# Retention, one core: the last head's totals and the first two tiles of the output projection in another order on TensorE

## The reference

```
def _mixer_retention(h, cos, sin, w_in, w_out):
    q, k, v, g = jnp.split(h @ w_in, SPLIT_RET, axis=-1)
    ...
    o = (scores of q and k, weighted by a decay) @ v, for 4 heads of 512 values
    ...
    o = _rms_noaffine(o).reshape(B, T, 2 * D_MODEL).astype(h.dtype)
    return (jax.nn.silu(g) * o) @ w_out
```

## Time and profile before

| what | us |
|---|---|
| three timed runs, median (lowest, highest) | 3081.69 (3080.63, 3082.3) |
| the profiled execution, its own time | 3077.38 |
| its span in the profile | 3075.6 |
| TensorE's matrix products, busy | 2896.1 (94%) |
| VectorE, ScalarE busy | 1446.9, 1105.1 |
| mean granted clock of TensorE | 0.968 |

### The profile page before, as it was taken

How to read it: one execution, slowest core, us unless ns; L and a number is a source line. 1 busy time by engine, 2 the same in 40 slices (tenths; PEclk the granted TensorE clock), 3 DMA queues, 4 the chain that set the end, 5 groups by cost and what they waited for, 6 DMA issues and landing times. The chain is left out here.

```text
span 3075.6 us, 38790 instructions
## 1 busy us (share of the span) xinstructions
PE 2896.1 (94%) x16100; PEld 2445.9 (80%) x16100; DVE 1446.9 (47%) x1607; ACT 1105.1 (36%) x1511; POOL 85.7 (3%) x92
## 2 busy tenths in 40 slices
PE   8898999999999899999898968899999999899999
PEld 7788999998986678888676767688887787678887
DVE  5664333233424544445466745544545765543322
ACT  5443332222232224332354434433223336444321
POOL 0000000002200000000000010000002000000000
PEclk9899999999999999999999989999999999899999
DMA  4212332323221135556322221355555221033322
GB/s 128 66 42 69 95 93 75 93 83 103 68 82 56 55 84 158 154 153 191 106 82 69 69 42 42 107 152 162 166 170 114 82 96 32 14 96 95 91 85 84
DMA packets 409375, 292.65 MB, mean 95 GB/s; under 512 B 24851, under 2 KB 388180, under 8 KB 409250
## 3 DMA queue, kind: packets, MB, share of 16 engines
q1 hardware_dynamic: 403210, 286.68, 32.1%
q0 software_dynamic: 1600, 3.55, 0.8%
q10 hardware_dynamic: 4440, 0.64, 0.2%
HBM read 286.16 MB, written 4.13 MB: 94 GB/s over the span
## 5 line engine op out<-in xcount | busy, mean ns | idle before, releaser
L197 DVE TENSOR_TENSOR w_lo<-w_raw,w_hi 128x2048 fp32r<-128x2048 f32 (+3 forms) x237 | 498.8, 2104 | 525.3 <-ACT w_hi L191 524.8
L191 ACT ACTIVATE w_hi<-w_raw 128x2048 fp32r<-128x2048 f32 (+3 forms) x237 | 416.1, 1756 | 259.0 <-PE ps L272 151.7
L270 PE MATMUL ps<-ffn_h_hi,w_hi 128*128 128x264 f32 (+1 forms) x1056 | 341.3, 323 | 6.6 <-DVE ffn_h_lo L380 6.6
L272 PE MATMUL ps<-ffn_h_hi,w_lo 128*128 128x264 f32 (+1 forms) x1056 | 340.4, 322 | 0.0
L271 PE MATMUL ps<-ffn_h_lo,w_hi 128*128 128x264 f32 (+1 forms) x1056 | 340.4, 322 | 0.0
L270 PE MATMUL ps<-up_act_hi,w_hi 128*128 128x512 f32 (+1 forms) x880 | 309.5, 352 | 0.0
L271 PE MATMUL ps<-up_act_lo,w_hi 128*128 128x512 f32 (+1 forms) x880 | 308.9, 351 | 0.0
L272 PE MATMUL ps<-up_act_hi,w_lo 128*128 128x512 f32 (+1 forms) x880 | 308.8, 351 | 0.0
L270 PE MATMUL ps<-up_h_hi,w_hi 128*128 128x512 f32 x704 | 279.5, 397 | 8.0 <-DVE up_h_lo L382 7.1
L271 PE MATMUL ps<-up_h_lo,w_hi 128*128 128x512 f32 x704 | 279.3, 397 | 0.0
L272 PE MATMUL ps<-up_h_hi,w_lo 128*128 128x512 f32 x704 | 278.8, 396 | 0.0
(11 more groups left out here) (543 smaller groups left out, 5410.3 us busy)
## 6 DMA issues: line engine op xcount, KB each, us to landing
mod_raw<-in_w_ada_dram SPq DMA_DIRECT2D x128, 384.0 KB, 3.9
w_raw<-in_ffn_w_gu_dram SPq DMA_DIRECT2D x88, 512.0 KB, 5.2
w_raw<-in_w_ffn_in_dram SPq DMA_DIRECT2D x88, 512.0 KB, 5.2
w_raw<-in_ret_w_in_dram SPq DMA_DIRECT2D x24, 1024.0 KB, 5.2
w_raw<-in_ffn_w_down_dram SPq DMA_DIRECT2D x32, 704.0 KB, 4.8
w_raw<-in_w_ffn_out_dram SPq DMA_DIRECT2D x32, 704.0 KB, 4.8
w_raw<-in_dsw_w_in_dram SPq DMA_DIRECT2D x18, 1024.0 KB, 5.0
w_raw<-in_gdn_w_in_dram SPq DMA_DIRECT2D x16, 1024.0 KB, 5.7
```

The costliest lines, as they stand in the source:

```text
L191: self.nc.scalar.activation(self.w_hi[:, s, 0:w.size], self.raw[:, s, 0:w.size], ACT.Copy).then_inc(self.hi_ready, 1)
L197: self.nc.vector.tensor_tensor(self.w_lo[:, s, 0:w.size], self.raw[:, s, 0:w.size], self.w_hi[:, s, 0:w.size].bitcast(F32), ALU.subtract). ...
L270: nc.tensor.matmul(out, w_hi, h_hi, start=first, stop=False)
L272: return nc.tensor.matmul(out, w_lo, h_hi, start=False, stop=last)
```

## The change

Only TensorE's program changes. The total of head 3 moves from ahead of head 4's four groups to behind the first of them. The total of head 4 moves from ahead of the projection to its row 6. The first two tiles of the projection are taken together: rows 0 to 11 of tile 0, then rows 0 to 11 of tile 1, then rows 12 to 15 (the rows of head 4) of tile 0, then those of tile 1. Each of the rows 12 to 15 waits for itself alone, where before there was one wait for four. The pair has no wait for free PSUM.

```diff
@@ add_projected, TensorE
                                     row_ready(pe, part * w.rows + k)
                                 mm = product(m, s, k)
                     mm.then_inc(K.tile_used, 1)
-            if side is None:
+            def first_pair(i, last):
+                for k0, k1 in ((0, before.LATE), (before.LATE, w.rows)):
+                    for j in range(2):
+                        pe.wait_ge(K.lo_ready, K.tile_no(w, i, j) + 1)
+                        hi, lo = K.weights(w, j, K.w_hi), K.weights(w, j, K.w_lo)
+                        for k in range(k0, k1):
+                            if j == 0:
+                                before.row_ready(pe, k)
+                            at = slice(cols[0] - base, cols[0] - base + wd)
+                            mm = split_products(nc, K.ps[:, j, 0:wd], hi[:, k, 0:P], lo[:, k, 0:P], src[0][:, k, at],
+                                                src[1][:, k, at], k == 0, k == w.rows - 1)
+                        if k1 == w.rows:
+                            mm.then_inc(K.tile_used, 1)
+            if isinstance(before, RetentionHeads):
+                K.over_tiles_peeled(pe, w, first_pair, trip)
+            elif side is None:
                 K.over_tiles_peeled(pe, w, first, trip)
             else:
                 first(0, False)
@@ RetentionHeads
+    LATE = NV * (RET_HEADS - 1)
+
     def row_ready(self, pe, row):
-        if row % self.NV == 0:
+        if row == self.LATE // 2:
+            self.total(pe, RET_HEADS - 1)
+        if row >= self.LATE:
+            pe.wait_ge(self.S["lo"], row + 1)
+        elif row % self.NV == 0:
             pe.wait_ge(self.S["lo"], row + self.NV)
+
+    def total(self, pe, h):
+        K, nc = self.K, self.K.nc
+        pe.wait_ge(self.S["summed"], h + 1)
+        if h:
+            pe.wait_ge(self.S["std"], h)
+        nc.tensor.matmul(K.ps[:, 7, :], K.ones[:], self.sq[:, 0, :], start=True, stop=True).then_inc(self.S["total"], 1)
@@ RetentionHeads.tensor
             if h + 1 < RET_HEADS:
                 scores(h + 1)
-            if h:
-                total(h - 1)
+            if 0 < h < RET_HEADS - 1:
+                self.total(pe, h - 1)
             for m in range(NV):
                 e = h * NV + m
                 bank = 5 + e % 2
+                if m == 1 and h == RET_HEADS - 1:
+                    self.total(pe, h - 1)
                 if e >= 2:
                     pe.wait_ge(S["gated"], e - 1)
...
                 mm.then_inc(S["out"], 1)
-        total(RET_HEADS - 1)
```

More of the change, by code:

```diff
@@ L1946, in scores @@
             mm.then_inc(S["scores"], 1)
-        def total(h):
-            pe.wait_ge(S["summed"], h + 1)
-            if h:
-                pe.wait_ge(S["std"], h)
-            nc.tensor.matmul(K.ps[:, 7, :], K.ones[:], self.sq[:, 0, :], start=True, stop=True).then_inc(S["total"], 1)
         scores(0)
```

## The result

Slower by a third of a per cent, as forecast. Eight timed runs of each kernel gave medians of 3090.64 us (3086.56 to 3093.82) for the changed kernel and 3080.47 us (3077.75 to 3082.3) for the one before: +10.2 us, ratio 1.0034 with a 95% interval of [1.0025, 1.0042], where 3090.0 and +8.3 us were forecast. That the time itself is only 0.6 us off is partly luck: the difference is 1.9 us larger than forecast, and the kernel before has a median 1.2 us lower over eight runs than over the three that the forecast started from. When it was timed again, beside the last experiments, it stood at 3089.06 against 3079.38 us, ratio 1.0033 [1.0020, 1.0045].

The account below looks back on a forecast made before the run. It took the chain from head 4's total to tile 1's weights as the bound. Terms -0.5 - 0.95 + 6.1 + 2.15 + 1.5 = +8.3 us on a 3081.7 us median gave 3090.0 us, range 3085.5 to 3093.5.

Parts of the forecast that it names:

- The paths that met at 1041.1: Start of tile 1: TensorE finishing tile 0 and the chain to tile 1's low weight half end almost together, at 1041.1.
- Total of head 3: Behind head 4's first group: shorter idle may keep TensorE's clock up and the total shorter, -0.5 us.
- Total of head 4: Behind six rows of tile 0: a short wait keeps full clock, so the root comes earlier, -0.95 us.
- The stall: Before tile 1's early rows: TensorE waits about 8.7 us for the low weight half, made after all of head 4.
- The hand-over: From tile 0 to tile 2, sharing a weight slot: only 12 late products cover it, 3.3 us bare; term +6.1 us.
- The clock behind the stall: At tile 1: TensorE comes back at 1.2 GHz after standing, costing 1.3 to 2.8 us, mean +2.15.
- The clock behind tile 2: After the 3.3 us wait at tile 2: possible half clock, bounds 0 and 3.0, taken as +1.5 us.
- Rival B: Whole stretch: the order costs as forecast but the clock hardly, +5.5 us, 3087.2 us, within 0.2%; 12 in 100.
- Rival A: At tile 1: low half is there when asked, no stall, tile 2 starts earlier, -4.2 us, 3077.5 us; 3 in 100.
- the signs named ahead: Retention's end and projection: two long idles, roots 1.2 us after totals, half clock 3 to 6 us, last addition 8 us later.
- the dropped wait for free PSUM: At the tile pair: costed at nothing, since its two banks held scores that were read long before.
- the single waits of the late rows: Tile 0's late rows: four waits costed at nothing, all met by the stall; without it at most 0.6 us saved.

Follow-up runs that it names:

- e6: Kernel before with only tile 1's weight halves written early, during head 1: 3081.00 us against 3079.42, ratio 1.0002.
- e3: Changed kernel with four rows of tile 1, not twelve, ahead of tile 0's late rows: 3082.63 us against 3080.34 for the kernel before.
- e7: Changed kernel with tile 1's halves early, eight rows of tile 1 first, both totals as before: 3079.47 us against 3079.42 for the kernel before.
- e4: Changed kernel with unread products in the waits before tile 1 and tile 2: 3086.91 us against 3080.34 for the kernel before.
- e10: Changed kernel with unread products only in the wait before tile 1: 3085.54 us against 3079.38 for the kernel before.
- e8: Changed kernel with eight rows of tile 1, not twelve, ahead of tile 0's late rows: 3085.47 us against 3079.42 for the kernel before.
- e9: Changed kernel run and profiled again, nothing altered: 3089.06 us against 3079.38 for the kernel before, ratio 1.0033.
- e2: Changed kernel with both weight halves of tile 1 written during head 1: 3076.80 us against 3080.34 for the kernel before.
- e1: Changed kernel with totals moved, but tile 0 and tile 1 one after the other: 3079.50 us against 3080.34 for the kernel before.

## Why the prediction was right, step by step

*The paths that met at 1041.1.* Right, and e6 shows it from the other side: with the weight half out of the way, nothing was gained.

*Total of head 3, -0.5 (bounds 0 and -0.92).* This step failed, and in more than its size. Its root stands 2.11 us behind the total (1012.46 - 1010.35), as before: 0 us. The 2.75 us of idle brought the clock down here and in seven of the eight experiments that have this hole (all but e3; e6 and e7 keep the longer one). But a full clock would not have paid what I priced it at either. In e3 the total ran at full clock, and its root came 1.16 us behind it (1009.39 - 1008.23); yet head 4's last addition of squares starts 17.20 us after head 3's, where that is 17.27 us before and 17.26 after:

```profile
1007.48 0.69 DVE L2074 TENSOR_TENSOR ret_sq<-ret_sq 128x512 f32<-128x512 f32 x1
1024.68 0.69 DVE L2074 TENSOR_TENSOR ret_sq<-ret_sq 128x512 f32<-128x512 f32 x1
```

```profile
1009.39 0.69 ACT L2005 ACTIVATE ret_rs<-ps,eps 128x512 f32<-128x512 f32 x1 [3.02 <-PE ps L1945]
```

TensorE, earlier there by a microsecond, waited 2.25 us for VectorE's gating, ran head 4's third group at half clock (its first row, at 1014.07, stands in the last section), and ScalarE's square of that group waited for it. Of the 0.95 us at the root 0.07 us reached the additions. My bound of -0.92 took the gain at the root for a gain at the end of the chain, though the text beside it has VectorE and ScalarE setting the pace; what a full clock throughout would bring, no run shows.

*Total of head 4, -0.95.* Root 1.17 us behind the total in place of 2.11: -0.94. The wait in front of it is 1.09 us, 1.3 forecast.

*The stall, 8.7 us.* It measured 8.66 us.

*The hand-over, +6.1.* With the clock kept up (e4, e10) the stage is +5.26; with the 0.94 added back, 6.2 us. The bare part at tile 2 is 3.15 us, 3.3 forecast. This is the main term, and e8 and e3 take it away in two steps.

*The clock behind the stall, +2.15.* It was at half for 5.5 us and more, in e9 too. From tile 1's first product to the addition for tile 0 it is 14.16 us in the changed kernel (1041.61 to 1055.77) and 14.25 in e9, where e4 and e10, at full clock, take 11.63: 2.5 and 2.6 us.

*The clock behind tile 2, +1.5 (bounds 0 and 3.0).* From tile 2's first product to its addition it is 14.41 us in the changed kernel's profile, 12.89 in e9's, and 11.62 in e4 and e10: 2.8, 1.3 and 0 us. Both bounds were nearly met, and the middle is about the mean of the three; which of them a run gets is luck.

The sum in the first profile is -0.94 + 6.2 + 2.5 + 2.8 = 10.56 where I had 8.3. The difference lies in the two terms for which I had only bounds, total 3 (0.5) and tile 2 (1.3), in the stall's clock (0.4) and in the hand-over (0.1). The advice of the Trainium skill, given there for thin M, to finish all K tiles before a wait ("TensorE: Matmul & The Clock Gate", section "HAM oscillation — how this bites in real kernels") would have given 9.8, nearer to this profile and to the timed +10.2; e10 shows that it is not always paid. Rival B's +5.5 is near what e4 and e10 measured, but by other terms: they had total 3 at half clock and none behind the stall. Rival A's condition was made in e2. For tile 2's start -4.2 us and the bare wait were forecast, and it came 4.0 us earlier (40.27 us after the start of the stage, 44.28 before); the stage is only 2.38 us shorter, since tile 2 then ran 3.4 us at half clock, 1.6 us of loss that the forecast of A left out.

Of the signs named ahead, two did not come as written: head 3's root stood 2.1 us behind its total and not 1.2, and the last addition came 12 us later and not 8, of which 1.4 us were there before the stage.

One thing that I argued and didn't test by itself: that the dropped wait for free PSUM and the single waits of the late rows cost nothing. No run puts them back alone; e4's stage, +5.26 us where the terms without the clock give +5.15, leaves them about 0.1 us.

## What to carry to other kernels

Before a tile is started early to fill a hole, ask who makes its operands and what that engine has to do first: here the second tile's weight half stood behind the very rows that the interleaving was to hide, and the late rows, ready, waited behind it. Price a gain on one step of a chain only as far as the next wait that other engines set: 0.95 us at a root was 0.07 us at the additions. Interleaving two tiles also brings the end of the first next to the end of the second, so a double-buffered slot gives its hand-over (6.2 us here) only the tail of the second as cover; leave enough of the second tile behind the first one's end. And a wait that moves onto the critical path brings its slow start with it: keeping TensorE busy took half of the loss away (5.3 of 10.6 us) in the profiles compared.

## What the runs showed of the hardware

An idle time of TensorE between about 2.25 and 3.2 us was followed by either clock. The hole of 2.75 us ahead of head 3's total is the same in nine profiles. In eight of them the total ran at half clock; in e3 it ran at full clock, which the first row shows by its 1.13 us (2.07 or 2.08 in the other kernels). The second row is also e3's, 3.6 us of products further on: after 2.25 us of idle the group ran at half clock (1.98 us, where it takes 1.12 or 1.13 in the other eight), where an idle of about the same length in the kernel before had left the clock up. The third is e10's start of tile 2.

```profile
1008.23 1.13 PE L1945 MATMUL ps<-ret_sq,ones 128*128 128x512 f32 x2 [2.75 <-DVE ret_sq L2074]
1014.07 1.98 PE L1994 MATMUL ps<-ret_p,ret_v 128*128 128x512 f32 x2 [2.25 <-DVE ret_gate L2055]
```

```profile
1056.74 0.49 PE L270 MATMUL ps<-ret_y_hi,w_hi 128*128 128x512 f32 x1 [3.16 <-DVE w_lo L197]
```

After 3.15 and 3.16 us before tile 2 the clock was at half twice (the changed kernel, e9) and at full once (e10). In e2, after 2.92 us, it fell only when TensorE had been running again for a microsecond:

```profile
1048.80:1049.80 1.00, 1.00 (x5) 0.82 (x5) 0.30 (x2) 0.70 (x2) 0.00 (x0) 0.99 0.05 15
1049.90:1053.30 3.40, 3.40 (x10) 2.67 (x9) 2.29 (x2) 1.63 (x1) 0.00 (x0) 0.52 1.01 282
1053.40:1056.00 2.60, 2.60 (x13) 2.11 (x12) 0.46 (x1) 0.00 (x0) 0.00 (x0) 1.00 0.33 74
```

Waits of 2.08 and 2.44 us (e1) left it up, those of 8.66 us brought it down in all four profiles that have one (the changed kernel twice, e3, e8). At tile 2 alone this luck is worth 0 to 2.8 us of a run. It may be why timings differ from the stage's sums by 1 or 2 us, but that is only argued from its size: no run fixed the clock in all stages. What decides between the two clocks after such an idle, these runs don't show.
